# Attention steps on TensorE: the transpositions of the step before the last stand ahead of the logits and of the values

## The reference

```python
def softmax_attn(q, k, v):
    s = jnp.einsum('bgrqd,bgkd->bgrqk', q, k).astype(jnp.float32) * SCALE
    p = jax.nn.softmax(s, axis=-1).astype(v.dtype)
    return jnp.einsum('bgrqk,bgkd->bgrqd', p, v)

def na_latent(q, k, v, k_ctx, v_ctx, bias, row_idx):
    ...
    s_win = jnp.einsum('bhrwd,bhrjud->bhrwju', qg, kg).astype(jnp.float32) * SCALE + bias[None]
    ...
    p = jax.nn.softmax(jnp.concatenate([s_win, s_ctx], axis=-1), axis=-1).astype(v.dtype)
    ...
    o = jnp.einsum('bhrwju,bhrjud->bhrwd', p_win, vg) + jnp.einsum('bhrwl,bhld->bhrwd', p_ctx, v_ctx)
```

## Time and profile before

| | |
|---|---|
| time, median of 3 runs | 2485.15 us (2484.32 to 2493.12) |
| profiled execution, first to last instruction (its span) | 2487.8 us |
| PE busy in the span | 2424.4 us (97%) |
| DVE busy | 1558.7 us (63%) |
| ACT busy | 1222.0 us (49%) |
| POOL busy | 363.5 us (15%) |
| chain that ended last: share on PE | 88% |

### The profile page before, as it was taken

One profiled execution on the slowest core, in us unless ns is written; L12 is line 12 of the kernel. 1 busy time (PEld: TensorE's weight loads), 2 busy tenths in 40 slices (PEclk: granted clock), 3 DMA queues, 4 the chain that ended last, 5 costly groups with the idle time before them and its releaser, 6 DMA issues.

```text
span 2487.8 us, 36743 instructions
## 1 busy us (share of the span) xinstructions
PE 2424.4 (97%) x14470; PEld 2065.6 (83%) x14470; DVE 1558.7 (63%) x2659; ACT 1222.0 (49%) x2224; POOL 363.5 (15%) x340
## 2 busy tenths in 40 slices
PE   8999999999999999999999999999999999999998
PEld 6855678878888877888888899998888888999887
DVE  5234345664456445667678768667867866757875
ACT  4334443422222535566556555466656654547653
POOL 0332422100001304310000000240000000024000
PEclk9999999999999999999999999999999999999999
DMA  6345113343444322345565563345455454335544
GB/s 273 137 152 187 52 68 119 137 175 138 152 170 160 136 88 95 124 163 191 166 213 186 168 190 127 129 169 186 176 184 200 176 183 164 132 114 195 192 169 137
DMA packets 88603, 390.05 MB, mean 157 GB/s; under 512 B 15024, under 2 KB 27600, under 8 KB 58352
## 3 DMA queue, kind: packets, MB, share of 16 engines
q1 hardware_dynamic: 81232, 356.17, 41.2%
q0 software_dynamic: 7200, 31.52, 3.5%
HBM read 386.62 MB, written 1.05 MB: 156 GB/s over the span
## 4 chain that ended last, share of the span: by engine, by line
PE 88%; ACT 5%; DVE 5%; issue 1%; DMA 0%; POOL 0%; SPq 0%; DVEq 0%; ACTq 0%; POOLq 0%
PE ps L1171 39%; PE ps L1211 36%; PE ps L1399 3%; PE ps L1476 2%; DVE ring_lo L2122 2%; PE ps L1461 2%; ACT logits L1858 1%; PE ps L1450 1%; ACT w_hi L1625 1%; PE ps L1302 1%; ACT prob_t L1865 0%; DMA arena<-w_mod 0%; PE ps L1411 0%; PE ps L1271 0%; PE ps L1239 0%
## 5 line engine op out<-in xcount | busy, mean ns | idle before, releaser
L2122 DVE TENSOR_TENSOR ring_lo<-ring,w_hi 128x1024 fp32r<-128x1024 f32 (+4 forms) x708 | 773.6, 1121 | 222.5 <-ACT w_hi L1625 220.1
L1625 ACT ACTIVATE w_hi<-ring 128x1024 fp32r<-128x1024 f32 (+4 forms) x708 | 634.2, 944 | 266.5 <-PE ps L1171 177.7
L1171 PE MATMUL ps<-h_hi,w_hi 128*128 128x256 f32 (+1 forms) x1632 | 500.6, 332 | 3.5 <-issue 1.6
L1171 PE MATMUL ps<-h_lo,w_hi 128*128 128x256 f32 (+1 forms) x1632 | 489.5, 326 | 1.5 <-DVE h_lo L2295 1.5
L1211 PE MATMUL ps<-h_hi,w_hi 128*128 128x512 f32 x1760 | 447.1, 393 | 2.2 <-DVE h_hi L2295 1.8
L1211 PEld LDWEIGHTS ps<-h_hi,w_hi 128*128 128x128 f32 x1760 | 316.8, 189 | 58.9 <-issue 2.8
L1171 PEld LDWEIGHTS ps<-h_hi,w_hi 128*128 128x128 f32 x1632 | 309.0, 191 | 40.5 <-issue 13.1
L1171 PEld LDWEIGHTS ps<-h_lo,w_hi 128*128 128x128 f32 x1632 | 309.4, 191 | 26.7 <-DVE h_lo L2295 1.7
L1171 PE MATMUL ps<-h_hi,ring_lo 128*128 128x256 f32 (+1 forms) x1632 | 304.6, 324 | 2.5 <-DVE ring_lo L2122 2.5
L1171 PEld LDWEIGHTS ps<-h_hi,ring_lo 128*128 128x128 f32 x1632 | 250.3, 190 | 27.3 <-DVE ring_lo L2122 3.0
L1211 PEld LDWEIGHTS ps<-h_hi,ring_lo 128*128 128x128 f32 x1760 | 243.0, 191 | 21.4 <-DVE ring_lo L2122 3.5
(11 more groups left out here) (298 smaller groups left out, 2920.5 us busy)
## 6 DMA issues: line engine op xcount, KB each, us to landing
ring<-w_ffn_in SPq DMA_DIRECT2D x132, 1024.0 KB, 4.8
ring<-w_ffn_out SPq DMA_DIRECT2D x96, 704.0 KB, 4.0
ring<-w_in SPq DMA_DIRECT2D x36, 1024.0 KB, 4.8
ring<-w_w_in SPq DMA_DIRECT2D x26, 1024.0 KB, 4.9
bias_t<-w_mod POOLq DMA_DIRECT2D x24, 1024.0 KB, 5.3
ring<-w_mod SPq DMA_DIRECT2D x16, 1024.0 KB, 6.9
ring<-w_up SPq DMA_DIRECT2D x16, 576.0 KB, 3.7
ring<-w_pab SPq DMA_DIRECT2D x8, 1024.0 KB, 4.8
```

The costliest lines, as they stand in the source:

```text
L1171: mm = pe.matmul(ps[fs[k].bank][:, at_col:at_col + n], (hi_w if wpart == "hi" else lo_w)[0:rows, at[k]:at[k] + P], hi if part == "hi" else ...
L1625: act.activation(w_hi[q.s % 2][:, h * n:(h + 1) * n], ring[q.slot][:, h * n:(h + 1) * n], ACT.Copy)\
L2122: dve.tensor_tensor(ring_lo[q.slot][:, c], ring[q.slot][:, c], plain(w_hi[q.s % 2][:, c]), ALU.subtract)\
```

## The change

In `pe_att`, and only there, the call of `turn` moves from the end of the item to its start. Nothing else is changed: the same instructions run on every engine, and DVE, ACT, POOL and SP keep their order.

```diff
@@ -1478,12 +1478,12 @@
                                            skip_group_check=True)
                     mm.then_inc(psum_full[f.bank], 1)
 
+                if 2 <= at < len(steps) + 2:
+                    turn(at - 2)
                 if at < len(steps):
                     scores(at)
                 if at >= 3 and steps[at - 3]["t"] == 1:
                     values(at - 3)
-                if 2 <= at < len(steps) + 2:
-                    turn(at - 2)
```

## The result

The changed kernel takes 2504.57 us (median of 5 runs, 2502.76 to 2507.79) against 2487.15 us of the kernel before, measured beside it (2484.32 to 2493.12): 1.0069 times as long, with an interval of 1.0058 to 1.008. That is +17.4 us, 0.7%. It is slower, and it lies outside the range of 2473 to 2491 us.

The account below looks back on a forecast made before the run. TensorE (PE), busy 2424.4 of 2487.8 us, was taken as the bound, so only its idle time could be won. Terms -1.5 - 0.8 - 0.5 - 0.7 = -3.5 us gave 2481.6 us against the median 2485.15; range 2473 to 2491 us.

Parts of the forecast that it names:

- kept the clock as it was: Whole kernel: the sum assumed an unchanged granted clock; a fall again around the head norms would give 2486.7 us.
- around the head norms: First stage: fewer waits -1.2, one logits product longer +1.0, DVE wait gone -0.6; sum -0.8 us.
- small waits: First stage, between 177 and 240 us: some small PE waits taken as gone, an estimated -0.5 us.
- six pairs: First stage, back to back pairs behind 240 us: +0.35, -0.65, 0, +0.5, -0.45, -0.45, together -0.7 us.
- second stage: Waits in odd items go, -2.6 us; +2.0 given back at the start, -0.9 at the end; sum -1.5 us.
- third and fourth stage: Idle time before the last values stays and product chunks between items cover the rest: 0 us.
- the odd items' period: Second stage: an odd item should repeat every 11.8 us, PE's own work, instead of 12.25 us.
- the second case: Rival, odd items: logits idle behind waiting transpositions if GpSimd ends over 11.8 us behind them; +11 us, 2496 us; chance 0.17.
- The 2.0 us of the sum: Second stage's start: logits held behind transpositions waiting for GpSimd, and again in the first odd item, 2 x 1.0 us lost.
- the 0.9 us more: Second stage's end, where no product chunks remain: the chain, ahead by about 1 us, ends the stage 0.9 us earlier.
- The gain of 2.6 us: Second stage, odd items: the wait before the values goes, 6 x 0.44 us.
- Case 5: Rival: the clock falls once more or for longer, +1.7 to +5.1 us, 2483 to 2487 us; chance 0.10.

Follow-up runs that it names:

- experiment 9: Changed kernel with the logits of eleven first-stage items issued once more, unread, ahead of waiting transpositions: 2497.36 us, 1.0039 of the kernel before.
- experiment 6: Changed kernel, but the second item of each of the first stage's six back to back pairs keeps the old order: 2496.0 us, 1.0027 of the kernel before.
- experiment 5: Changed kernel, but items 7 to 13 of the first stage, around the head norms, keep the old order: 2494.94 us, 1.0027 of the kernel before.
- Experiment 10: Kernel before reordered to logits, transpositions, values in every item, with eight small unread products in two items around the head norms: 2483.51 us, 0.9988 of it.

## Why the prediction was wrong

Two steps failed. The sum let the transpositions wait ahead of the logits at almost no price; and it kept the clock as it was. Term by term, between fixed products on PE (the first from the first reciprocal; the last column takes 0.5 us off for each slow us more):

| term of the sum, us | forecast | measured | at full clock |
|---|---|---|---|
| around the head norms, to 213.9 us | -0.8 | +7.6 | +2.4 |
| small waits, to 238.2 us | -0.5 | 0.0 | 0.0 |
| six pairs, to 325.9 us | -0.7 | +3.2 | +1.5 |
| second stage | -1.5 | -0.7 | -0.7 |
| third and fourth stage | 0 | +2.1 | +2.1 |

**What held.** In the second stage the waits before the values went, GpSimd became a releaser, DVE waits for logits instead of transpositions, and the odd items' period is 11.91 us for a forecast of 11.8. That no wait for GpSimd came in between was closer than the sum says: GpSimd's step ended 971.67 + 3.11 - 962.58 = 12.2 us behind the start of the transpositions, where the forecast had 11.7 and the second case put its limit at 11.8. Head 1's transpositions start only 0.5 us behind head 0's, which neither number took in, and so they were 0.2 us behind its end. PE's order of transpositions ahead of values is worth what rows 5 promised and more: -3.0 us in that stage where the odd items alone are turned around, -4 to -8 us at full clock in the first.

**The even items, and every item behind another: the step that failed.** The prediction counted an even item as one group of transpositions moved past 1.06 us of logits, and let it cost something only at the second stage's start (2.0 us) and in the pairs. Alone it costs 2.9 us in the second stage (1.2 if the slow time there is taken off), 0.9 in the third, and 213.6 - 207.8 = 5.8 us in the first. The timeline of the changed kernel at the start of the second stage shows how:

```profile
938.29 0.66 PE L1461 MATMUL ps<-con,logits 128*128 128x128 f32 x4 [1.34 <-POOL logits L2049]
...
939.83 0.66 PE L1461 MATMUL ps<-con,logits 128*128 128x128 f32 x4 [0.89 <-POOL logits L2049]
...
940.42 1.13 PE L1450 MATMUL ps<-arena 64*128 64x512 f32 x4
```

The logits could have run in these 2.2 us and stand behind them. The 2.0 us of the sum were right for this place (2.6 us measured up to the product that stands at 942.21 us before and at 954.60 after, less the 9.8 us that the kernel is late there anyway); the 0.9 us more that it took off at the end did not come as such. The gain of 2.6 us was read too high: of the six waits of the earlier trace rows one is the 1.5 us at the stage's end, and the five others come to 2.1 us; over the five periods 1.8 us were won. -1.5 was forecast, -0.7 measured from the first to the last reciprocal, and -0.25 with the values and transpositions behind the last one (between the products at 924.00 and 1020.49 us before, 933.81 and 1030.05 after). In the third and fourth stages the same thing happens once, at the first even item, whose second group of transpositions waits 0.99 us: the forecast said 0 since product chunks lie between the items, and overlooked that GpSimd starts from nothing there.

**The pairs**. -0.7 us for the six was forecast; on PE's timeline, product to product, they lost about 3 us, half of it by the clock. The same pair in the changed kernel:

```profile
248.65 2.36 DVE L2122 TENSOR_TENSOR ring_lo<-ring,w_hi 128x1024 fp32r<-128x1024 f32 x2 [1.83 <-ACT w_hi L1625]
248.74 1.03 PE L1461 MATMUL ps<-con,logits 128*128 128x128 f32 x8
...
249.71 1.13 PE L1450 MATMUL ps<-arena 64*128 64x512 f32 x4
...
251.00 0.67 DVE L2517 TENSOR_SCALAR_CACHE_REDUCE logits<-ps 128x512 f32<-128x512 f32 x1
...
253.40 0.58 ACT L1865 ACTIVATE prob_t<-ps 128x512 f32<-128x512 f32 x1
...
254.12 1.09 PE L1461 MATMUL ps<-con,logits 128*128 128x128 f32 x8 [2.27 <-ACT prob_t L1865]
...
255.14 2.08 PE L1450 MATMUL ps<-arena 64*128 64x512 f32 x4
...
257.25 0.69 DVE L2517 TENSOR_SCALAR_CACHE_REDUCE logits<-ps 128x512 f32<-128x512 f32 x1 [1.96 <-PE ps L1450]
```

The first transpositions end at 249.7, but ACT copies them out only at 253.40: in the order of the items its copy stands behind the exponentials of the same item's logits, these behind DVE's subtraction, and DVE splits weights (line 2122) until 251.0. Moving the transpositions ahead brings the copy 0.6 us forward, against the end of the product (253.98 - 248.74 = 5.24 us, 249.65 - 243.79 = 5.86 before). The next transpositions need that copy, the next logits only DVE's subtraction, done by 251.7 for the first head. Before, the logits ran in between (from 247.40); now they come behind. Their banks come free first, so they belong first. For this pair the sum had +0.35 us and it cost +1.5, of which 1.0 is the logits product at half the clock (2.08 us instead of 1.06). The wait's end, 5.4 us behind the start, was where the sum had it, only released by ACT and not by GpSimd. For the others the sum had -0.65, 0, +0.5, -0.45, -0.45; they gave +0.15, +0.9, +0.9, -0.2, -0.2. In experiment 9, where the clock stays up here, the six give +0.5, -0.4, +0.9, +0.9, -0.2, -0.2.

The kernel of experiment 6 shows what the second item's order alone costs. With it as before, and the first item turned around, the first, second, fifth and sixth pair take 0.8, 1.7, 1.0 and 1.0 us *less* than in the kernel before, with no slow time in them; in these the second item is an even one. With it turned around too they take 0.5 more, and 0.5, 0.2 and 0.2 less, at full clock. In the third and fourth pair the second item is an odd one: 0.05 (3.4 slow us taken off) and 0.2 more with it as before, 0.9 more each with it turned around. So each of the six pays 0.7 to 1.3 us for logits behind a wait that they used to run in, 5.6 us together, which is nearly all of the 5.8 us by which experiment 6 shortens the first stage. The first items of the pairs, turned around, win 4.3 us.

**Around the head norms.** -0.8 and -0.5 us were forecast. Up to the head sums about 0.7 us were won; then came waits of the transpositions for four different things: the head norm's bank emptied by ACT (line 1840), ACT's copy, the head norm's bank emptied by DVE (line 2474), and the rotary product's (line 2484):

```profile
159.53 1.06 PE L1461 MATMUL ps<-con,logits 128*128 128x128 f32 x8 [0.86 <-ACT arena L1840]
...
165.55 1.39 PE L1461 MATMUL ps<-con,logits 128*128 128x128 f32 x8 [2.05 <-ACT prob_t L1865]
166.88 1.23 PE L1450 MATMUL ps<-arena 64*128 64x256 f32 x4
```

```profile
192.89 0.63 PE L1461 MATMUL ps<-con,logits 128*128 128x128 f32 x4 [0.93 <-DVE arena L2474]
193.45 1.12 PE L1450 MATMUL ps<-arena 64*128 64x256 f32 x4
```

```profile
209.80 0.63 PE L1461 MATMUL ps<-con,logits 128*128 128x128 f32 x4 [1.64 <-DVE arena L2484]
210.36 0.97 PE L1450 MATMUL ps<-arena 64*128 64x256 f32 x4
```

The second, for ACT's copy, is the one that the sum had. The other three were not in it at all: banks 5 and 6 are shared with the head norms and the rotary product, whose results are taken out late, and logits and values covered that before. Around the first two the kernel lost 2.2 us, around 192.89 us 2.6, around 209.80 us 2.8, the slow clock behind them included.

**The clock.** "My sum keeps the clock as it is" failed with the largest part. The first stage has 13.6 slow us more (6.8 us of time), and the fall ahead of 1088 us is 3.4 us longer (1.7 us). Over all runs the direction is the same: mean granted clock 0.9884 in the five of the changed kernel, 0.9936 in 76 of the kernel before, and among executions of one kernel 0.001 less clock goes with 1.6 us more (a straight line through 186 runs of twelve kernels, one level for each kernel). At equal clock the changed kernel would be 9 us slower by that line, not 17; the two profiles, with 13.5 slow us between them at 0.5, leave 13.2 - 6.7 = 6.5 us. By both about half is order and half clock. With 0.5 us for each of the 26 slow us that lie between the two mean clocks (0.0052 x 2 x 2490), only 4 of the 17.4 us would be order. All three are estimates. Case 5 named this mechanism and gave it 1.7 to 5.1 us and a chance of 0.10: too small in both. Four of the five falls start 0.7 to 0.9 us behind the start of a group of transpositions that came out of a wait (165.55, 192.89, 209.80, 254.12 in the rows above; falls at 166.3, 193.6, 210.7, 255.0). The other way round it does not hold. In the first stage thirteen such groups came out of a wait of over 0.8 us, and behind two of the three longest no fall came:

```profile
290.69 1.06 PE L1461 MATMUL ps<-con,logits 128*128 128x128 f32 x8 [2.91 <-ACT prob_t L1865]
...
303.65 0.63 PE L1461 MATMUL ps<-con,logits 128*128 128x128 f32 x4 [2.21 <-ACT prob_t L1865]
```

In experiment 5 the same two groups came out of waits of 2.91 and 2.22 us, at 281.22 and 295.78, and there both were followed by a fall (282.2 and 295.8). So it is not the order and the wait alone that decide. With unread products put into those waits, experiment 9 had two falls instead of five.

The Trainium skill (TensorE: Matmul & The Clock Gate, Part 4: PE-mode transpose) says that transpositions don't count as busy time for the clock in the way that other products do. The prediction held the steady clock of the second stage against that rule (with transpositions in sixteen of its items, not fourteen). The four places fit it, but no run here separates it from the plain wait. In experiment 5 the logits (163.41 us, wait 0.92) and the values (165.51, wait 0.88) came out of the waits, the transpositions only behind them at 168.56, and the clock fell at 166.1 us all the same; in the second stage of the changed kernel transpositions came out of waits of 1.34, 0.89, 0.87 and 1.06 us, and the granted clock stayed at 1.00. What the runs show is that more and longer waits went with more slow time, and experiment 9 that filling them brought most of it back. Experiment 10 is the caution: there filling waits did not help.

**The second case** (the queue behind the transpositions, 2496 us) was the right side, in the wrong items: it put the price on odd ones, which together are better off by the change (-3.0 us in the second stage, -3.8 in the first at full clock). That the time at equal clock would lie near its 2496 us is luck: the places and the sizes are others.

What stays open: what makes the clock fall behind one wait and not behind another, and why the same instructions draw 3.4, 6.8 or 10.2 slow us.

## What to carry to other kernels

When independent groups of work on an in-order engine have to be ordered, put first the group whose inputs and banks come free first, and last the one that nobody waits for: here logits, then transpositions, then values. Read for each group what it waits for and what would have run in that wait, once for every kind of item and for every other user of its banks; a kind that looks like "moved by one product" can lose all that the other kind wins. A wait can also cost the clock: in the first stage here the slow time cost more than the order itself (6.8 against 3.2 us). The rule of order is shown for this kernel's first two stages; in the last two, where PE hardly waits, it lost 0.8 us each.

## What the runs showed of the hardware

- The granted clock of the same instruction order in the first stage was at half for 10.2, 3.4 and 6.8 us in three executions, and for 13.6 and 6.8 us in two of another order. Each such us cost 0.44 us in the first three (0.57 in the other two, 3.85 / 6.8).
- 22 unread products more made a kernel 7 us faster (2504.57 to 2497.36 us); the granted clock was 0.99 instead of 0.95 in the first stage, and at full clock both stages come to the same (211.5 and 211.0 us).
- Four of thirteen groups of transpositions behind waits of 0.86 to 2.91 us were followed by a fall of the clock of 3.4 us within 0.9 us of their start; behind the two waits of 2.91 and 2.21 us none was.
- 57.69 us for the third stage with the values last, against 56.93 with the transpositions last: where PE is bound by its own work, the order that wins elsewhere loses 0.8 us.
